# First layer's output panels interleaved, the compression MLP placed among the window-key units with 128 stationary columns, the last query rotation placed inside a softmax, two last panels exchanged

## The reference

```python
h = x
for i in range(2):
    hn = rms_norm(h, ln_mix_pre[i])
    m = gla_mla_mixer(hn, ...) if i == 0 else nsa_mixer(hn, ...)
    h = h + rms_norm(m, ln_mix_post[i])
    f = swiglu(rms_norm(h, ln_ffn_pre[i]), ...)
    h = h + rms_norm(f, ln_ffn_post[i])
    h = h + sigmoid(h @ ple_w_gate[i] + ple_b_gate[i]) * (p[i] @ ple_w_proj[i])

# gla_mla_mixer ends with:  concatenate([o_gla, o_mla], -1) @ w_out
def nsa_compress(t, pos, w1, w2):        # t [groups 4, tokens 256, 128]
    blocks = t[:, :, idx, :] + pos       # 15 blocks of 32 tokens, for keys and for values
    return gelu(flat(blocks) @ w1) @ w2  # w1 [4096, 128], w2 [128, 128]
# nsa_mixer: rotary positions on queries and keys; compressed, selected and
# windowed attention over 16 heads in 4 groups; gates; then o @ w_out
```

## Time and profile before

| | before |
|---|---|
| time, median of 3 runs | 2486.06 us (2484.45 to 2490.2) |
| profiled execution, time | 2485.95 us |
| its span in the profile | 2484.2 us |
| PE busy | 2443.7 us (98%) |
| DVE, ACT busy | 1349.6 us (54%), 1045.3 us (42%) |
| DMA, 16 engines, mean | 181 GB/s, 448.95 MB |
| chain that ended last, share of PE | 96% |

### The profile page before, as it was taken

One profiled execution on the slowest core, in us unless ns is written; L12 is line 12 of the kernel. 1 busy time (PEld: TensorE's weight loads), 2 busy tenths in 40 slices (PEclk: granted clock), 3 DMA queues, 4 the chain that ended last, 5 costly groups with the idle time before them and its releaser, 6 DMA issues.

```text
span 2484.2 us, 29267 instructions
## 1 busy us (share of the span) xinstructions
PE 2443.7 (98%) x11694; PEld 2051.4 (83%) x11694; DVE 1349.6 (54%) x1219; ACT 1045.3 (42%) x1003; POOL 21.0 (1%) x39
## 2 busy tenths in 40 slices
PE   7999999999999999999999999999999999999999
PEld 7887788888888888888888888878888888888887
DVE  4655646444445444457675576565444445444575
ACT  5444345333333333345443354453333333334453
POOL 0000100000000000000000000000000000000000
PEclk9999999999999999999999999999999999999999
DMA  7554356555555555556555632456555555555564
GB/s 227 187 162 136 128 182 220 187 186 190 199 187 186 191 199 187 177 178 220 186 174 163 212 119 85 157 173 200 186 187 197 192 186 186 196 193 182 177 217 136
DMA packets 226960, 448.95 MB, mean 181 GB/s; under 512 B 7961, under 2 KB 19233, under 8 KB 225586
## 3 DMA queue, kind: packets, MB, share of 16 engines
q1 hardware_dynamic: 225218, 440.72, 53.9%
q10 hardware_dynamic: 1648, 6.89, 0.7%
HBM read 445.48 MB, written 2.10 MB: 180 GB/s over the span
## 4 chain that ended last, share of the span: by engine, by line
PE 96%; DVE 2%; ACT 1%; issue 1%; DMA 0%; ACTq 0%; DVEq 0%
PE PG L533 87%; PE MB L533 1%; PE MB L639 1%; PE MB L853 1%; PE MB L517 1%; PE MB L657 1%; PE PG L1006 1%; PE MB L667 0%; ACT whl L1031 0%; DVE whl L1444 0%; PE MB L635 0%; DMA pp<-in_p 0%; PE PG L760 0%; PE PG L577 0%; PE PG L579 0%
## 5 line engine op out<-in xcount | busy, mean ns | idle before, releaser
L1444 DVE TENSOR_TENSOR whl<-raw,whl 128x2048 fp32r<-128x2048 f32 (+4 forms) x435 | 955.7, 2198 | 910.1 <-ACT whl L1031 910.0
L1031 ACT ACTIVATE whl<-raw 128x2048 fp32r<-128x2048 f32 (+4 forms) x435 | 800.9, 1841 | 1120.6 <-PE PG L533 1093.4
L533 PE MATMUL PG<-whl,XBh 128*128 128x512 f32 (+1 forms) x3376 | 798.7, 386 | 2.3 <-DVE XBl L1454 1.4
L533 PE MATMUL PG<-whl,XAh 128*128 128x512 f32 (+1 forms) x3136 | 747.3, 388 | 5.8 <-ACT rt L1268 2.7
L533 PEld LDWEIGHTS PG<-whl,XBh 128*128 128x128 f32 x3376 | 624.4, 188 | 128.1 <-DVE XBl L1454 1.7
L533 PEld LDWEIGHTS PG<-whl,XAh 128*128 128x128 f32 x3136 | 585.0, 189 | 121.8 <-ACT rt L1268 3.1
L533 PE MATMUL PG<-whl,XBl 128*128 128x512 f32 (+1 forms) x1688 | 412.5, 386 | 0.0
L533 PE MATMUL PG<-whl,XAl 128*128 128x512 f32 (+1 forms) x1568 | 384.2, 387 | 0.0
L533 PEld LDWEIGHTS PG<-whl,XBl 128*128 128x128 f32 x1688 | 313.2, 188 | 63.0
L533 PEld LDWEIGHTS PG<-whl,XAl 128*128 128x128 f32 x1568 | 292.7, 188 | 57.4
L1039 ACT ACTIVATE XBh<-MB 128x512 fp32r<-128x512 f32 (+1 forms) x34 | 18.5, 597 | 50.4 <-PE MB L517 49.3
(11 more groups left out here) (327 smaller groups left out, 1087.4 us busy)
## 6 DMA issues: line engine op xcount, KB each, us to landing
raw<-in_ffn_w_gate SPq DMA_DIRECT2D x88, 1024.0 KB, 5.1
raw<-in_ffn_w_up SPq DMA_DIRECT2D x88, 1024.0 KB, 5.1
raw<-in_ffn_w_down SPq DMA_DIRECT2D x64, 1024.0 KB, 5.0
raw<-in_nsa_w_in SPq DMA_DIRECT2D x36, 1024.0 KB, 5.0
raw<-in_ple_w_gate SPq DMA_DIRECT2D x32, 1024.0 KB, 5.0
raw<-in_ab_w_in SPq DMA_DIRECT2D x24, 1024.0 KB, 5.3
raw<-in_ffn_w_down SPq DMA_DIRECT2D x32, 768.0 KB, 4.3
raw<-in_ab_w_out SPq DMA_DIRECT2D x16, 1024.0 KB, 5.1
```

The costliest lines, as they stand in the source:

```text
L533: return mm(bank(m), X[x][:, chunk, m * P:(m + 1) * P], w[:, k, c * ncol:(c + 1) * ncol], start=x == 0 and w is wh and c == 0 and pos in ( ...
L1031: A(wh[:, place % 2, 0:w], raw[:, place, 0:w], ACT.Copy).then_inc(hi_ready, 1)
L1444: V.tensor_tensor(wl[:, k, 0:w], raw[:, place, 0:w], wh[:, k, 0:w].bitcast(F32), ALU.subtract).then_inc(lo_ready, 1)
```

## The change

1. **First layer's output.** Panels 0 and 1 are interleaved: `OUT0_UNITS` has both panels' MLA parts first, and after them the GLA parts. The transposes of the GLA output move from the gap after the second unit to the gap after the third, those of `pp` to the gap after the fifth. The DMAs of `pp` and `wbc` are issued earlier by ACT, ahead of the two squarings of GLA step 5 (line 1129 before).
2. **Compression MLP.** Slot SW1 is gone. SKW has 8 units: its four own units at even j and the four MLP units at odd j. `BL` gets 64 columns instead of 60 per part (the last 4 are set to zero by DVE), so that high and low part are 128 adjacent columns and one matmul takes both: 64 matmuls in place of 128, into bank 1 of `MB`. ACT and DVE copy the result to `GC`, PE adds its four quadrants and transposes by matmuls with the identity (6 in place of 2 transposes) in the gap after (SVS, 2), and the GELU runs on 128 partitions at the place of that gap. The second product moves to the gap after (SVW, 2).
3. **Split of the MLP's input.** The high part of `BL` is made one stage later on ACT, its low part two stages later on DVE, behind the evacuation.
4. **Last query rotation.** In the softmax of gap (SQ+3, 3) `meanwhile` is the evacuation of slot SQ+3; the low split that stood there is done in its regular place behind the softmax.
5. **Last panels.** Units (0,3) and (1,3) of the second layer's output are exchanged, and panel 1 is read out first.

```diff
-OUT_UNITS = (..., (2, 2), (0, 3), (1, 3), (2, 3))
+OUT_UNITS = (..., (2, 2), (1, 3), (0, 3), (2, 3))
+OUT0_UNITS = ((0, 0), (0, 1), (1, 0), (1, 1), (0, 2), (0, 3), (1, 2), (1, 3))
...
-                if (s, j) == (OUT0, 1):
+                if (s, j) == (OUT0, 2):
                     pe.wait_ge(go_ok, 1)
                     transpose_in(lambda c, m: gg[:, m, c * P:(c + 1) * P], 4, TQ["gla"], 4)
...
-                if (s, j) == (SW1 + 1, 2):
-                    pe.wait_ge(ge_ok, 1)
+                if (s, j) == (SVS, 2):
+                    pe.wait_ge(gc_a, 1)
+                    pe.wait_ge(gc_v, 1)
                     pe.wait_ge(tx_lo, TQ["p1"])
                     for kv in range(2):
-                        last = nc.tensor.transpose(MB[:, 0, 64 * kv:64 * kv + 60], GU[:, kv, :], ident[0:60, 0:60])
+                        o = MB[:, 0, 60 * kv:60 * kv + 60]
+                        mm(o, GC[:, kv, 0:P], ident[:, 0:60], start=True, stop=False)
+                        mm(o, GC[:, kv, 0:P], ident[:, 64:124], start=False, stop=False)
+                        last = mm(o, GC[0:60, kv, P:2 * P], ident[0:60, 0:60], start=False, stop=True)
...
-                    banks_free(s0)
-                    for j in range(4):
-                        if j == 0:
+                    for n, (panel, part) in enumerate(OUT0_UNITS):
+                        if n == 0:
                             pe.wait_ge(att_v, MLA_STEPS + 2)
-                        if j >= 2:
-                            pe.wait_ge(tx_lo, TQ["gla"] + 2 * j - 2)
-                        unit(s0, j, XB)
-                        gap(s0, j)
+                        if part == 0:
+                            banks_free(OUT0 + panel)
+                        if part >= 2:
+                            pe.wait_ge(tx_lo, TQ["gla"] + 2 * part - 2)
+                        unit(OUT0 + n // 4, n % 4, XB, par=(OUT0 + panel) % 2, pos=part)
+                        gap(OUT0 + n // 4, n % 4)
...
-                        if s == SW1:
-                            kv, k, buf = j // 2, j % 2, U.place(s, j) % 2
+                        if s == SKW and j % 2:
+                            kv, k, buf = j // 4, j // 2 % 2, U.place(s, j) % 2
...
-                                for part in range(2):
-                                    last = mm(PG[0:60, s % 2, kv, 0:2 * P], BL[:, kv, 16 * k + l, part, :],
-                                              whl[:, :, buf, l * P:(l + 1) * P],
-                                              start=(k == l == part == 0), stop=(k == part == 1 and l == 15))
+                                last = mm(MB[:, 1, 2 * P * kv:2 * P * kv + 2 * P],
+                                          BL[:, kv, 16 * k + l, :, :].rearrange("p a n -> p (a n)"),
+                                          whl[:, :, buf, l * P:(l + 1) * P],
+                                          start=(kv == k == l == 0), stop=(k == 1 and l == 15), skip_group_check=True)
...
                 if k == 5:
                     act.wait_ge(go_ps, 1)
+                    act.dma_start(pp[:, :, :], p_d[0]).then_inc(pp_in, 16)
+                    act.dma_start(wbc[:, :], T["ln_mix_post"][0:1, :].broadcast_to([P, D])).then_inc(wbc_in, 16)
...
-                        nsa_stage(g, lambda: split_once(x // 4, x % 4))
+                        nsa_stage(g, (lambda: evac(SQ + 3)) if k == (SQ + 3, 3) else lambda: split_once(x // 4, x % 4))
...
-                if (s, j) == (OUT1, 0):
-                    evac(s - 1)
...
+                if (s, j) in ((SVC + 1, 1), (SKS + 1, 1)):
+
+                    n = s - SVC - 1
                     v.wait_ge(bh_ok, n + 1)
-                    v.wait_ge(bt_ok, n + 1)
-                    V.tensor_tensor(BL[:, n, :, 1, :], BT[:, :, :], BL[:, n, :, 0, :].bitcast(F32),
+                    V.memset(BL[:, n, :, :, 60:64].bitcast(F32), 0.0)
+                    V.tensor_tensor(BL[:, n, :, 1, 0:60], BT[:, :, :], BL[:, n, :, 0, 0:60].bitcast(F32),
                                     ALU.subtract).then_inc(bl_ok, 1)
...
-                    mixer_panel(0, U(OUT1 + 2) + 2)
+                    mixer_panel(1, U(OUT1 + 2) + 2, 0)
                     for j in range(4):
                         split(OUT1 + 3, j)
                         if j < 2:
-                            mixer_panel(1 + j, U(OUT1 + 2) + 3 + j)
+                            mixer_panel(2 * j, U(OUT1 + 2) + 3 + j, 1 + j)
```

More of the change, by code:

```diff
@@ L43 @@
 L1 = FFN0 + FFN_SLOTS + 6
-SKC, SVC, SKS, SW1, SKW, SVS, SVW, SGT, SQ, OUT1 = (L1 + i for i in (0, 1, 2, 3, 4, 5, 6, 7, 8, 12))
+SKC, SVC, SKS, SKW, SVS, SVW, SGT, SQ, OUT1 = (L1 + i for i in (0, 1, 2, 3, 4, 5, 6, 7, 11))
 FFN1 = OUT1 + 6
@@ L108, in units @@
 def units(s):
-    return 1 if UQN <= s < KG or any(s in p for p in PROJ) else 4
+    return 1 if UQN <= s < KG or any(s in p for p in PROJ) else 8 if s == SKW else 4
 BASE = [0]
@@ L121, in staged @@
     plan = {}
-    for slots in (range(QG, OUT0 + 1), range(L1, OUT1 + 3)):
+    for slots in (range(QG, OUT0 + 2), range(L1, OUT1 + 3)):
         run = [(s, j) for s in slots for j in range(units(s))]
@@ L409, in _ @@
                 if layer == 0:
-                    for n in range(4):
-                        k_units(OUTS[0] + n, ab_out, 512 * n, c0=8)
+                    for n, (panel, part) in enumerate(OUT0_UNITS):
+                        c = (8 + 4 * part) % KC
+                        unit(OUT0 + n // 4, n % 4, ab_out[:, c:c + 4, 512 * panel:512 * panel + 512], 4, 512)
+                    for n in (2, 3):
+                        k_units(OUT0 + n, ab_out, 512 * n, c0=8)
                 else:
@@ L928, in _ @@
                         gap(OUT1 + n // 4, n % 4)
-                for s in range(s0 + 1 + 2 * layer, s0 + 4):
-                    banks_free(s)
+                for s in range(s0 + 2 + layer, s0 + 4):
+                    banks_free(s if layer == 0 else OUT1 + 2)
                     for j in range(4):
@@ L1251, in _ @@
             norm_sums(0)
-            for s in range(1, OUT0 + 1):
+            for s in range(1, OUT0 + 2):
                 for j in range(units(s)):
@@ L1910, in _ @@
                 if layer == 0:
-                    with v.Fori(0, 3) as i:
+                    mixer_panel(0, U(OUT0 + 1) + 2)
+                    for s in (OUT0 + 2, OUT0 + 3):
                         for j in range(4):
-                            split(i + (s0 + 1), j)
+                            split(s, j)
                             if j == 1:
-                                mixer_panel(i)
+                                mixer_panel(s - OUT0 - 1)
                 else:
-                    mixer_panel(0, U(OUT1 + 2) + 2)
+                    mixer_panel(1, U(OUT1 + 2) + 2, 0)
                     for j in range(4):
```

105 lines of the change are left out of this document (56 added, 49 removed).

## The result

The changed kernel takes 2464.71 us (median of 4 runs, 2464.47 to 2466.65) against 2487.89 for the kernel before beside it (2484.45 to 2490.20): a ratio of 0.9913, 95% interval 0.9899 to 0.9926. Its profiled execution took 2466.65 us (span 2464.8), the longest of the four. The forecast was 2463.8 us, range 2459 to 2470.

A forecast was written before the change was run, and what follows sets the result against it. PE, busy 98% of the span, bounds the kernel, so only its work, waits and clock can give time. Gains 3.3 + 8.2 + 6.1 + 4.5 = 22.1 us off the profiled 2485.95 gave 2463.8 us, range 2459 to 2470.

The forecast's parts named there:

- first layer's output: Interleaved panels of the first layer's output: 4.1 us of PE waits go, 0.8 charged; gain 3.3 us (2.4 to 4.1).
- compression MLP: MLP units among the key units: 19.1 us go, 7.7, 0.5 and 2.7 come back; gain 8.2 us (4.5 to 11).
- last rotation: Last query rotation ahead of the softmax: 3.55 us of wait and 2.6 of clock; gain 6.1 us (3.5 to 6.4).
- last panels: Fourth panel of the second layer's output: 2.87 us of wait and 1.68 of clock; gain 4.5 us (3.5 to 4.6).
- DVE's late split: First layer's output, third unit: low split stands behind the GLA output on DVE; 0.8 us charged, with 0.1 for ACT's queue.
- The DMA issues: First layer: two issues ahead of the squarings hold ACT by under 1 us; 0.1 charged for ACT's queue.
- the wait for KB: SKW, behind the first MLP unit: PE waits 1.4 us for the SKS keys that DVE rotates.
- the price of that drop: First 64 old MLP matmuls at a clock of 0.82: 8.86 - 7.51 = 1.35 us.
- the small products: Gap after (SVS, 2): six at 0.106 us each in place of two cheap transposes add 0.5 us (0 to 0.8).
- A new wait also costs clock: Rival: the 1.4 us wait in SKW lowers the clock, with a second drop in the first layer +3 to +5; chance 0.13.
- Loads pace: Rival: each of 64 wider MLP matmuls waits for its 192 ns load, 12.3 us instead of 7.7, 2468.4 us; chance 0.03.
- The mixed slot is smoother: Rival: DVE gets to rotation and splits earlier, the 2.7 and 0.8 us fall away, 2460.3 us; chance 0.09.

The follow-up runs named there:

- the second set of runs: The changed kernel run again in the first group, beside the kernel before: median 2465.00 us against 2486.3 us.
- part undone: Changed kernel with one part put back: first layer's output 2470.06 us, compression MLP 2472.19, last rotation 2471.16, last panels 2470.29.
- the folded kernel: Changed kernel with SKS key transposes and BL's low part for the values later, and one small product with matrix `fold` for two: 2464.87 us.
- the narrow one: Changed kernel, MLP units still interleaved, but high and low part as two matmuls of 60 stationary columns, 4 small products for 6: 2468.70 us.
- the undone kernel: Changed kernel with second-layer output units (0,3) and (1,3) in their old order and panel 0 read out first: 2470.29 us.
- a second ordering: Changed kernel with SKS key transposes one unit later and BL's low part for the values two stages later on DVE: 2465.20 us.
- the first group: The runs of the kernels with parts undone, the changed kernel (2465.00 us) and the kernel before beside them (median 2486.3 us).
- the kernel without the 85 us wait: Changed kernel with low-rank inputs' transposes in four banks of MB instead of two, gate inputs' transposes in a PG bank: 2464.34 us.

## Why the prediction was right

The sum came out at 22.1 us; the rows give 3.4 + 7.4 + 6.0 + 4.5 = 21.3 for the same four stretches, and the medians 23.2, or 21.3 in the second set of runs.

| term | forecast | rows of before and after | part undone, medians | fastest runs |
|---|---|---|---|---|
| first layer's output | 3.3 | 33.61 - 30.16 = 3.4 | 5.1 | 2.9 |
| compression MLP | 8.2 | 142.16 - 134.80 = 7.4 | 7.2 | 7.1 |
| last rotation | 6.1 | 6.0 | 6.2 | 5.6 |
| last panels | 4.5 | 2.87 + 1.68 = 4.5 | 5.3 | 2.6 |

The medians of undone parts hold differences from elsewhere, as said at each; the rows are the measure. The forecast time is the sum taken off one execution of the kernel before. That it lies 0.9 us from the median measured is partly luck, since the medians of the kernel before moved from 2486.1 to 2487.9 us between its first three runs and all four.

*First layer's output.* As forecast, to the wait: 0.8 us were charged for DVE's late split, and it is 0.49 plus the lag of the pipeline, 307.18 against 301.09 + 5.45 = 306.54, so 0.6. The DMA issues held ACT as expected, and DVE's next split hid it.

*Compression MLP.* The matmuls are 16 in 1.92 us and 120 ns apart, the waits come to 33.06 - 4 x 5.45 - 7.7 - 0.9 = 2.7 us where I counted 2.7, and the wait for KB is where it was put, 1.16 for 1.4. Two terms were mis-sized. The 8.86 us of the earlier trace rows are the length of the stretch that I cut, and it ends before the first 64 matmuls do; they take 9.14, so 19.4 us go in place of 19.1, and the price of that drop is 9.14 - 7.51 = 1.6, not 1.35. The chain of the kernel before:

```profile
1292.14 9.14 PE PG L1006 x64
```

The other is the small products. I charged 0.106 us for each, but the 16 of the earlier trace rows are matmuls, two to a float32 product: line 760 makes 2 x 4 = 8 products. Six products are 12 matmuls, 1.27 us at that price, and they took 1.78. Less the 0.25 of the two old transposes that is 1.5 in place of 0.5, outside my bound of 0.8. Half of the 1.0 too little is the count, and what makes the other half stays open: 0.15 us for each matmul here, 0.166 in the folded kernel (8 in 1.33 us), 0.129 in the narrow one, where all have 60 rows (8 in 1.03 us). The fold's 0.45 for four matmuls fewer is 0.11 each, the ordinary price. With both, 19.4 - 7.7 - 1.5 - 2.7 = 7.5, against 7.4 in the rows.

*Last rotation.* From the end of the unit to the first score product 1527.46 - 1518.44 = 9.02 us before, 1512.49 - 1509.46 = 3.03 after: 6.0 for 6.1. The wait kept is 0.3 with the lag, as charged, and the step put behind, the low split, held nobody up.

*Last panels.* The wait is gone and the four units take 21.77 us. The number agrees with the trace of before, but the undone kernel shows that the 1.68 of it belongs to executions in which the clock fell. My term was right for the profile that I made the sum against, and too firm as a term of the median.

*The rivals.* "A new wait also costs clock" did not happen behind the 1.2 us wait in either trace of the changed kernel. "Loads pace" is refuted by 120 ns starts with 192 ns loads. A load of 60 columns takes 131 ns in the kernel before:

```profile
L1006 PEld LDWEIGHTS PG<-whl,BL x128: 129/131/220, 1292.1 to 1309.3; 128*60 128x60 f32 x128
```

The Trainium skill's rule (TensorE: Matmul & The Clock Gate, LDWEIGHTS) has the load's time in proportion to the columns. Here it grows with them, but 192 is 1.5 times 131 and not twice, and the product doesn't wait for the load at 256 moving columns. "The mixed slot is smoother" did not come: the waits are the 2.7 us counted, and the 0.8 of the first layer is 0.6.

*What I had not in the range's reasons.* The prediction says that five waits are over 1.3 us besides that for the first inputs. The same view of the kernel before has three more: 2.2 us near the start, 1.4 near 239 us, and this one near 85 us.

```profile
PE MB L517 <- DVE XBl L1459: 1.5, 1, 1.5
```

The change leaves it alone, and the clock falls behind it in some executions. The profiled execution after was 2466.65 us, 1.9 above the median of its kernel; 1.6 of that is the drop near 85 us, absent from the profile of before, and 0.25 a later start of the transposes there. The trace-to-trace difference, 19.3 us, is the 21.3 less this, to 0.1 us. A reader who had only the two profiles would have found 2 us missing and looked for them in the change.

## What to carry to other kernels

Where PE sets the time, list all its waits with the granted clock behind each, also those that the change leaves alone: filling a wait of 3.7 us gave 6 us, and moving a few instructions of another engine ahead of or behind each other was enough. Before a matmul stream is shortened, write down the other engines' order beside it, since short units uncover their splits: here 2.7 of the 11 us freed went back into such waits, and a second ordering won 1.4 of them. Compare single edits of this size in the rows of the stretch, or within executions with the same clock history, not by medians alone.

## What the runs showed that I had not expected

A wait of a given length does not fix what the clock does. The 1.5 us wait near 85 us stands in the traces of 12 executions. The clock fell behind it in seven and not in the five others, and in the changed kernel in one of two (first 8 matmuls 3.35 or 2.09 us, 1.6 us in all). Behind 2.7 us it fell in one of three traces of one kernel (3.51 or 2.11 us), and in the kernel before; behind 2.6 us at the MLP and behind 3.7 us in both traces that have that wait; behind 1.9 and 1.4 us at the GLA output in none of two.

Nor does it take a wait just before. In every trace here the clock is at 0.50 for 3 us or more near 262 us, behind 16 matmuls of two columns in the GLA steps (line 720), and the last wait of PE ahead of it, 1.4 us, ended some 20 us earlier. It is there before and after, so it cancels, except in the first trace with the panels' order undone, where it lasted over 6 us and cost 1.6 us more.

The kernel before, with three long waits, spanned 2484.2 to 2490.7 us in the nine runs of the first group (2481.5 to 2491.7 over all three), the changed kernel 2464.7 to 2467.2, and the kernel without the 85 us wait 2464.0 to 2465.0. That fits scatter which comes from what the clock does behind waits; it is not shown, as only one execution of the kernel before was traced, and the first 84 us scatter by 1.2 us as well, with a recorded clock of 1.00.
